# Raw fp32 weights in place of split halves for the second block's projections: a two-block transformer kernel on one Trainium2 core

## Chip, cores and metric

The kernel runs on one core of one Trainium2 chip. The metric is the device time of one execution in microseconds (us). The engines are called as in the profile: PE is TensorE's matmul stream and PEld its weight loads, DVE is VectorE, ACT ScalarE, POOL GpSimd, and SP the queue of SyncE, which issues the loads of the weights.

## What is computed

A batch of one sequence of 256 tokens with 1024 features goes through two different blocks, all in float32. The first block has two layers of attention and a convolved, gated MLP. The second block normalises its input and projects it with one wide matrix, `w_in_2`, and everything that follows in it reads slices of that product:

```python
xn = rmsnorm(h, norm1_g[layer])
proj = xn @ w_in[layer]
u, q, k, v, qi, ki, wi, g_ssm, g_attn = jnp.split(proj, offsets, axis=-1)
y_ssm = s5_branch(u, ...)              # a linear recurrence over the tokens, 512 features
y_attn = dsa_branch(q, k, v, qi, ki, wi)   # attention over keys chosen by an index score
merged = sigmoid(g_ssm) * (y_ssm @ w_ssm_up) + sigmoid(g_attn) * (y_attn @ w_attn_up)
h = h + merged @ w_out
h = h + peer_ffn(rmsnorm(h, norm2_g), ...)   # product-key routing to 16384 experts
```

The widths of the slices are 512 (u), 512 + 128 + 128 (q, k, v), 256 + 32 + 8 (qi, ki, wi) and twice 1024 (the gates).

## The kernel before

**Units.** Every weight matrix is cut into units of 128 x 1024 float32 (512 KB), listed in `plan` in the order of use. A unit has a slot, `i % 6`, with three buffers of SBUF: `raw` (what SP loads), `wh` and `wl`. ACT copies `raw` into `wh` as float32r (L953), and DVE (L1284) or POOL (L1941) writes the rest, `raw - wh`, into `wl`; the table `lower` says which of the two. The activations have the same two halves: after a transposition on PE, ACT copies the bank into `hh`, and DVE subtracts (L1290) into `hl`. `mm3` (L507) then multiplies each pair with three float32r matmuls: high by high, high by low, low by high.

**Who waits for whom.** SP loads unit i into `raw` when the unit six places ahead has had its low half made (L470 on). ACT writes `wh` again when PE has used the unit six places ahead. The three engines that split do it inside their own programs, in order: each `stream(i)` in such a program is the place where it splits the units that have come free, and what stands behind it on the engine waits too.

**The stage around the change.** It runs in the profile from about 720 to 900 us. First come the two RMS norms between the blocks (DVE at L1639 and L1650, roots on POOL), the transposition `turned(("n", 2), ...)` (L523) and `by_features("u", ...)`: 4 units, each of 8 products with 256 moving columns. DVE prepares `Br`, PE turns it (L745), and DVE and ACT copy it into `BT`. Then a loop over n = 0 to 15 does the recurrence, one step for 32 features. In its step n PE does `state_in(n + 1)` (L498, four records with 32 rows), `state_out(n - 1)` (L780, eight records), some transpositions of queries and index scores (n = 7 to 11), and then `FILL[n]` units of the projections `wqkv` (8 units), `wqk` (one unit, 16 products of 40 columns) and `wga` (16 units). A unit of `wqkv` or `wga` holds four products with 512 moving columns. Three units are left for after the loop, and `state_out(15)` stands behind them.

```python
FILL = [2, 2, 2, 2, 2, 2, 1, 2, 1, 1, 1, 1, 1, 1, 1, 0]
for n in range(16):
    if n + 1 < 16:
        state_in(n + 1)
    if n:
        state_out(n - 1)
    ...
    for _ in range(FILL[n]):
        next(fill)
run(fill)
state_out(15)
```

In step n DVE multiplies the bank of `state_in(n)` with a table, adds, and runs two scans (L1734); POOL multiplies the result (`ssb` or `ssv`, L1946), and that is what `state_out(n)` waits for. At n = 5 DVE also rotates queries and keys (`rope`, four products and two sums) and POOL the index queries, and from n = 10 DVE chooses keys (`chosen`, L1301, L1712, L1714). Behind its step DVE makes the low halves of as many units as `FILL[n]` says. ACT copies the finished projections out of their banks. After the stage, at 900.89 us, the attention over the chosen keys begins with a matmul on `qT`.

Of the kernel before, what the change touches and what calls it, by code (L numbers as in the profile page):

```python
# [8 lines left out]
F32R = mybir.dt.float32r  # L9
# [79 lines left out]
def tcols(t):  # L89
    return slice(t * 128, (t + 1) * 128)  # L90
# [5 lines left out]
def program(nc, x_d, pos_d, consts_d, smalls_d, win_d, wout_d, wup_d, wdown_d, rows_d, wu_d, wqkv_d, wqk_d, wga_d, wsm_d,  # L96
            wglu_d, wsu_d, wau_d, wout2_d, wpq_d, keys_d, ut_d, vt_d, out_d, spill_d):
    with ExitStack() as ctx:

        def scoped(where, name, n, dt=F32):  # L100
            return where.enter_context(nc.sbuf_tensor(name, [128, n], dt))
# [13 lines left out]
        whs += [scoped(early, f"wh{i}", 1024, F32R) for i in (4, 5)]  # L115
        wls += [scoped(early, f"wl{i}", 1024, F32R) for i in (4, 5)]
# [47 lines left out]
        def stage(name, units):  # L164
            first[name] = len(plan)
            plan.extend(units)

        def quarters(w):
            return [(w[:, h * 1024:h * 1024 + 1024], 1024, True) for h in range(w.shape[1] // 1024)]


        WOUT = [(0, 0), (0, 1), (1, 0), (1, 1), (0, 2), (1, 2), (0, 3), (1, 3)]
# [7 lines left out]
            stage(("wdown", L), [(wdown_d[L, f], 1024, True) for f in range(NTILE)])  # L180
        stage(("row", "g"), [(rows_d[4], 1024, False)])
        stage(("row", "n", 2), [(rows_d[5], 1024, False)])
        stage("wu", [(wu_d[n], 1024, True) for n in range(4)])
        stage("wqkv", quarters(wqkv_d[0]) + quarters(wqkv_d[1]))
        stage("wqk", [(wqk_d, 320, True)])
        stage("wga", sum([quarters(wga_d[n]) for n in range(4)], []))
        stage("wglu", [(wglu_d[n], 1024, True) for n in range(2)])
        stage("wsu", quarters(wsu_d[0]) + quarters(wsu_d[1]))
        stage("wau", quarters(wau_d[0]) + quarters(wau_d[1]))
# [28 lines left out]
        J_GATE, N_GR = 57, 64  # L218


        normed = [first["wup", L] for L in range(DEPTH)] + [first["win", 1], first["wu"], first["wpq"]]


        lower = []
        for i in range(n_units):
            d2 = first["wga"] - 8 <= i < first["wglu"]
            if i < 6:
                lower.append("pd"[i % 2])
            elif first["ut"] <= i < first["ut"] + J_GATE:
                lower.append("p")  # L230
            elif first["ut"] <= i < first["vt"]:
                lower.append("d")
            elif any(u <= i < u + 4 for u in normed):
                lower.append("p")
            elif i >= first["ut"]:
                lower.append("dp"[i % 2])
            elif i >= first["wpq"]:
                lower.append("dp"[i % 2])
            elif i >= first["wglu"]:
                lower.append("p")  # L240
            elif d2:
                lower.append("d")
# [20 lines left out]
        def lo_out(i):  # L263
            return dve_lo if lower[i] == "d" else pool_lo

        def unit_pair(i, k, kt, cols):
# [8 lines left out]
        hTl = hl[:, :].rearrange("p (k t) -> p k t", k=8)  # L275
        hn2 = att[:, 0:2048].rearrange("p (t d) -> p t d", t=2)
        cosT = tab_s[:, 0:4096].rearrange("p (n t) -> p n t", n=16)
        sinT = tab_s[:, 4096:8192].rearrange("p (n t) -> p n t", n=16)
# [14 lines left out]
        def hT(k, cols):  # L293
            return hTh[:, k, cols], hTl[:, k, cols]
# [189 lines left out]
        def pe(p):  # L484
# [31 lines left out]
            def turned(st, src, ncol, ts, after, of=range(8)):  # L516
                for t in ts:
                    for q in range(ncol // 4):
# [6 lines left out]
                        bank_of["T", st, t, q] = b  # L525
                        emptied[b] = (dve_out, ("hT", st, t, q))

            def by_tokens(tag, u0, n_slabs, cw, nu, kper, off, ready, empties, of=range(8), skew=(), between=None):
                for n in range(n_slabs):
                    bs = [rot(of), rot(of)]  # L530
                    order = [(h, t) for h in range(nu) for t in range(2)]
                    if n in skew:
                        order.sort(key=lambda ht: ht[1])
                    for h, t in order:
                        i, b = u0 + n * nu + h, bs[t]
                        if t == 0:
                            unit(i)
                        elif n in skew and h == 0 and between:
                            between()
                        if h == 0:  # L540
                            claim(b)
                        m = mm3(banks[b][:, 0:cw], [hT(off + h * kper + k, tcols(t)) for k in range(kper)],
                                [unit_pair(i, k, kper, slice(0, cw)) for k in range(kper)], h == 0, h == nu - 1,
                                lambda k: ready(t, h * kper + k))
                        if h == nu - 1:
                            bank_of[tag, n, t] = b
                            emptied[b] = empties(n, t)
                            m.then_inc(pe_out.up(("mm", tag, n, t), ("used", i) if t else None), 1)
                        elif t:
                            m.then_inc(pe_out.up(("used", i)), 1)  # L550
                        if t:
                            yield

            def by_features(tag, u0, n_slabs, kt, c2, off, ready, empties):
                for n in range(n_slabs):
                    i = u0 + n
                    unit(i)
                    for c in range(c2):
                        b = rot()
                        claim(b)  # L560
                        m = mm3(banks[b][:, 0:256], [unit_pair(i, k, kt, tcols(c)) for k in range(kt)],
                                [hT(off + k, ALLC) for k in range(kt)], True, True, ready)
# [7 lines left out]

            def ready_tokens(st):
                return lambda t, k: p.wait_ge(dve_out, ("hT", st, t, k // 4))

            def ready_both(st):
                return lambda k: p.wait_ge(dve_out, ("hT", st, 0, k // 4), ("hT", st, 1, k // 4))
# [173 lines left out]
            low, side = [0, 1, 2, 3], (2, 3)  # L749

            def projections():
                yield from by_tokens("wqkv", first["wqkv"], 2, 512, 4, 2, 0, ready_tokens(("n", 2)), lambda n, t: (act_out, ("ev", "wqkv", n, t)), of=low)
                yield from by_tokens("wqk", first["wqk"], 1, 40, 1, 8, 0, ready_tokens(("n", 2)), lambda n, t: (act_out, ("ev", "wqk", n, t)), of=low)
                low[:] = [0, 1]
                yield from by_tokens("wga", first["wga"], 4, 512, 4, 2, 0, ready_tokens(("n", 2)), lambda n, t: (act_out, ("ev", "wga", n, t)), of=low)

            fill = projections()

# [177 lines left out]
        def act(a):  # L936
# [335 lines left out]
        def dve(v):  # L1272
# [958 lines left out]
```

## Time and profile before

| | us |
|---|---|
| median of 3 runs | 1850.11 |
| lowest, highest | 1848.39, 1851.78 |
| time of the profiled execution | 1850.76 |
| its span (first to last instruction) | 1849.0 |
| PE busy | 1736.3 (94%) |
| DVE busy | 1192.5 (64%) |
| ACT busy | 870.2 (47%) |
| POOL busy | 744.6 (40%) |

The busy time of PE counts overlapping matmuls once, and each matmul's time includes its way through the array, so the time from one start to the next is the cost in a stream, and not the duration of one. A float32 matmul shows in the trace as two records.

### The profile page before, as it was taken

The numbers are of one execution on the slowest core, as the hardware profiler recorded it, in microseconds if no ns is written. First come the engines' busy times: TensorE is split into PE (matmuls) and PEld (weight loads), VectorE is DVE, ScalarE is ACT, GpSimd is POOL, SyncE is SP. The second block draws the span as 40 slices with busy tenths as digits, with TensorE's granted clock in tenths as the row PEclk, the third lists the DMA queues.
The fourth block names the chain that finished last, engine by engine and source line by source line (L and its number), as shares of the span: only waits on it lengthen the run. The fifth ranks groups of instructions, "written<-read, shape, count | busy, mean of one in ns | idle before, by whom it ended". The sixth has DMA issues, their size and how long they took to land.

```text
span 1849.0 us, 27364 instructions
## 1 busy us (share of the span) xinstructions
PE 1736.3 (94%) x10744; PEld 1513.6 (82%) x10744; DVE 1192.5 (64%) x2462; ACT 870.2 (47%) x1508; POOL 744.6 (40%) x398
## 2 busy tenths in 40 slices
PE   6998999989989998988788999989999999999997
PEld 4776999867679986765567999989999988888886
DVE  7453674745447666677653399989999844444444
ACT  5544566344456654222444355544444445555553
POOL 2323578043236752232445399830000044444442
PEclk9998999999999998989899999999999999999998
DMA  7231555553235565422134365644444456666664
GB/s 277 88 106 67 186 185 166 185 183 103 92 114 191 175 193 179 134 81 67 57 114 159 113 208 172 194 138 146 140 144 142 160 171 193 194 193 194 193 194 136
DMA packets 77456, 283.21 MB, mean 153 GB/s; under 512 B 8720, under 2 KB 8976, under 8 KB 77072
## 3 DMA queue, kind: packets, MB, share of 16 engines
q1 hardware_dynamic: 76032, 276.50, 46.2%
q10 hardware_dynamic: 1296, 4.97, 0.7%
q8 instruction: 85, 1.39, 0.3%
q14 instruction: 43, 0.35, 0.1%
HBM read 279.33 MB, written 2.10 MB: 152 GB/s over the span
## 4 chain that ended last, share of the span: by engine, by line
PE 76%; DVE 15%; issue 3%; ACT 3%; POOL 2%; DMA 1%; POOLq 0%; DVEq 0%; ACTq 0%
PE bank L507 66%; PE bank L498 7%; DVE H L1290 2%; POOL wl L1941 2%; PE bank L590 1%; DVE H L1815 1%; DVE H L1821 1%; DVE H L1817 1%; ACT wh L953 1%; DVE H L1819 1%; DVE H L1813 1%; PE bank L780 1%; DVE gates L1290 1%; DVE ssb L1290 1%; DVE wl L1284 1%
## 5 line engine op out<-in xcount | busy, mean ns | idle before, releaser
L1941 POOL TENSOR_TENSOR wl<-raw,wh 128x1024 fp32r<-128x1024 f32 x227 | 579.6, 2564 | 729.7 <-ACT wh L953 714.7
L953 ACT ACTIVATE wh<-raw 128x1024 fp32r<-128x1024 f32 x515 | 532.6, 1048 | 109.8 <-PE bank L507 99.8
L507 PE MATMUL bank<-hh,wh 128*128 128x256 f32 x1904 | 546.5, 287 | 5.8 <-DVE hl L1290 3.1
L507 PE MATMUL bank<-hl,wh 128*128 128x256 f32 x1904 | 538.5, 283 | 0.0
L507 PE MATMUL bank<-hh,wl 128*128 128x256 f32 x1904 | 537.0, 282 | 0.0
L1284 DVE TENSOR_TENSOR wl<-raw,wh 128x1024 fp32r<-128x1024 f32 (+1 forms) x288 | 382.9, 1335 | 144.8 <-ACT wh L953 144.7
L507 PEld LDWEIGHTS bank<-hh,wh 128*128 128x128 f32 x1904 | 364.5, 191 | 8.1 <-POOL wl L1941 5.6
L507 PEld LDWEIGHTS bank<-hl,wh 128*128 128x128 f32 x1904 | 364.6, 192 | 0.0
L507 PEld LDWEIGHTS bank<-hh,wl 128*128 128x128 f32 x1904 | 364.1, 191 | 0.0
L1290 DVE TENSOR_TENSOR acl<-H,ach 128x256 fp32r<-128x256 f32 x128 | 87.6, 685 | 183.2 <-ACT ach L956 183.2
L507 PE MATMUL bank<-wh,ach 128*128 128x512 f32 x512 | 200.0, 391 | 1.9 <-DVE acl L1290 1.9
L507 PE MATMUL bank<-wl,ach 128*128 128x512 f32 x512 | 199.9, 390 | 0.0
L507 PE MATMUL bank<-wh,acl 128*128 128x512 f32 x512 | 199.7, 390 | 0.0
L507 PE MATMUL bank<-wh,hh 128*128 128x512 f32 (+1 forms) x432 | 180.4, 418 | 9.8 <-DVE hl L1290 5.3
L956 ACT ACTIVATE H<-bank 128x256 f32<-128x256 f32 (+33 forms) x197 | 64.5, 327 | 247.6 <-PE bank L507 215.1
L507 PE MATMUL bank<-wl,hh 128*128 128x512 f32 (+1 forms) x432 | 172.3, 399 | 0.0
L507 PE MATMUL bank<-wh,hl 128*128 128x512 f32 (+1 forms) x432 | 172.2, 399 | 0.0
L956 ACT ACTIVATE ach<-H 128x256 fp32r<-128x256 f32 x128 | 53.4, 418 | 174.3 <-PE bank L507 173.8
L1301 DVE SCALAR_TENSOR_TENSOR att<-bank,sml,att 128x255 f32<-128x255 f32 (+1 forms) x176 | 84.5, 480 | 62.5 <-ACT att L956 59.4
L507 PEld LDWEIGHTS bank<-wh,ach 128*128 128x128 f32 x512 | 96.4, 188 | 22.4 <-issue 2.1
L507 PEld LDWEIGHTS bank<-wh,hh 128*128 128x128 f32 x432 | 84.6, 196 | 35.6 <-issue 11.6
L507 PEld LDWEIGHTS bank<-wh,acl 128*128 128x128 f32 x512 | 96.5, 189 | 20.2
(203 smaller groups left out, 2289.1 us busy)
## 6 DMA issues: line engine op xcount, KB each, us to landing
raw<-in_ut_dram SPq DMA_DIRECT2D x128, 512.0 KB, 3.5
raw<-in_vt_dram SPq DMA_DIRECT2D x128, 512.0 KB, 3.7
raw<-in_wup_dram SPq DMA_DIRECT2D x88, 512.0 KB, 4.0
raw<-in_win_dram SPq DMA_DIRECT2D x48, 512.0 KB, 4.5
raw<-in_wdown_dram SPq DMA_DIRECT2D x44, 512.0 KB, 4.1
raw<-in_wout_dram SPq DMA_DIRECT2D x24, 512.0 KB, 3.6
raw<-in_wga_dram SPq DMA_DIRECT2D x16, 512.0 KB, 3.5
raw<-in_wpq_dram SPq DMA_DIRECT2D x16, 512.0 KB, 3.6
```

Of the source, the lines that this page charges most:

```text
L498: m = p.e.matmul(out, l, r, start=i == 0, stop=i == len(pairs) - 1)
L507: m = p.e.matmul(out, lhs[i][a], rhs[i][b], start=start and i == 0 and j == 0, stop=stop and i == n - 1 and j == 2)
L590: m = p.e.transpose(banks[b][:, 128 * k:128 * k + 128], buf[:, 1024 + 256 * (i % NB) + 128 * k:1152 + 256 * (i % NB) + 128 * k], ids[:, :])
L780: m = p.e.matmul(banks[yb][o:o + 32, 0:256], l[:, 32 * n:32 * n + 32], s, start=j == 0, stop=j == 3, tile_position=(0, o))
L953: a.e.activation(high_of(u), raw_of(u), ACTF.Copy).then_inc(act_hi.up(("hi", u)), 1)
L956: a.e.activation(out, src, f, **kw).then_inc(act_out.up(ev), 1)
L1284: v.e.tensor_tensor(low_of(u), raw_of(u), high_of(u).bitcast(F32), ALU.subtract).then_inc(dve_lo.up(("lo", u)), 1)
L1290: v.e.tensor_tensor(out, a, b, op).then_inc(dve_out.up(ev), 1)
L1301: v.e.scalar_tensor_tensor(out, a, s, b, op0, op1).then_inc(dve_out.up(ev), 1)
L1813: v.e.max(values[:, 0:8], s_).then_inc(dve_out.up(), 1)
L1815: v.e.max_index(index[:, 0:8], values[:, 0:8], s_).then_inc(dve_out.up(), 1)
L1941: g.e.tensor_tensor(low_of(u), raw_of(u), high_of(u).bitcast(F32), ALU.subtract).then_inc(pool_lo.up(("lo", u)), 1)
```

## The change

The 29 units of `wu`, `wqkv`, `wqk` and `wga` are no longer split. PE multiplies `raw` itself, in float32, with the whole activation, which stands in a new buffer `hw` (view `hTw`). Each product is one float32 matmul in place of three float32r ones: 144 in place of 432. ACT's copies into `wh` and DVE's and POOL's subtractions of these units go away. Of the four copies of the activation from its banks, ACT does the two of the first half of the features and DVE the two of the second, without waiting for each other. A raw buffer of these units is free for the next load when PE has used the unit, not when it has been split. To make room, `hw` lies over `wh4` and `wl4`, and the slots are shifted by two so that slot 4 fits this. All other weights are split as before.

```diff
-            whs += ... (4, 5); wls += ... (4, 5)
...
+        whs += [scoped(sc_h, "wh4", 1024, F32R), wh5]
+        wls += [scoped(sc_h, "wl4", 1024, F32R), wl5]
+        sc_h.close()
+        hw = scoped(early, "hw", 2048)
...
-        stage("wu", [(wu_d[n], 1024, True) for n in range(4)])
-        stage("wqkv", quarters(wqkv_d[0]) + quarters(wqkv_d[1]))
-        stage("wqk", [(wqk_d, 320, True)])
-        stage("wga", sum([quarters(wga_d[n]) for n in range(4)], []))
+        stage("wu", [(wu_d[n], 1024, False) for n in range(4)])
+        stage("wqkv", quarters(wqkv_d[0], False) + quarters(wqkv_d[1], False))
+        stage("wqk", [(wqk_d, 320, False)])
+        stage("wga", sum([quarters(wga_d[n], False) for n in range(4)], []))
...
-        slot = [i % 6 if i < n_early else (i - n_early) % 4 for i in range(n_units)]
+        slot = [(i + 2) % 6 if i < n_early else (i - n_early) % 4 for i in range(n_units)]
...
         def used_by(i):
-            return dve_out if plan[i][0] is not None and not plan[i][2] and not first["keys"] <= i < n_early else pe_out
+            whole = first["wu"] <= i < first["wglu"] or first["keys"] <= i < n_early
+            return pe_out if plan[i][2] or whole else dve_out
...
+            def turned_whole(st, src):
...
+                        emptied[b] = (dve_out if q else act_out, ("hT", st, t, q))
...
+                            for k in range(kper):
+                                ready(t, h * kper + k)
+                                m = p.e.matmul(banks[b][:, 0:cw], hTw[:, off + h * kper + k, tcols(t)], unit_whole(i, k, kper, slice(0, cw)),
+                                               start=h == 0 and k == 0, stop=h == nu - 1 and k == kper - 1)
...
+                            for k in range(kt):
+                                ready(k)
+                                m = p.e.matmul(banks[b][:, 0:256], unit_whole(i, k, kt, tcols(c)), hTw[:, off + k, ALLC], start=k == 0, stop=k == kt - 1)
...
-            turned(("n", 2), hn2, 8, (0, 1), lambda t: (dve_out, ("nrm", ("n", 2), t)))
-            by_features("u", first["wu"], 4, 8, 1, 0, ready_both(("n", 2)), lambda c: (act_out if c % 2 else dve_out, ("ev", "u", c)))
+            turned_whole(("n", 2), hn2)
+            by_features("u", first["wu"], 4, 8, 1, 0, ready_whole_both(("n", 2)), lambda c: (act_out if c % 2 else dve_out, ("ev", "u", c)))
...
-            turned(("n", 2), (0, 1), 2)
+            for t in range(2):
+                a.wait_ge(pe_out, ("T", ("n", 2), t, 0))
+                do(hTw[:, 0:4, tcols(t)], quad(ps("T", ("n", 2), t, 0)), ACTF.Copy, ("hT", ("n", 2), t, 0))
...
-            turned(("n", 2), (0, 1), 2)
+            for t in range(2):
+                v.wait_ge(pe_out, ("T", ("n", 2), t, 1))
+                copy(hTw[:, 4:8, tcols(t)], quad(ps("T", ("n", 2), t, 1)), ("hT", ("n", 2), t, 1), alone=True)
```

## Rows read from the trace of the kernel before

**Rows 1.** The page: busy us of each engine, share, instructions.

```profile
PE 1736.3 (94%) x10744; PEld 1513.6 (82%) x10744; DVE 1192.5 (64%) x2462; ACT 870.2 (47%) x1508; POOL 744.6 (40%) x398
```

**Rows 2.** Windows: length, busy PE, PEld, DVE, ACT, POOL, granted clock, DMA share, GB/s.

```profile
750.00:760.00 10.00, 10.00 (x33) 7.37 (x34) 6.02 (x8) 1.06 (x1) 3.28 (x1) 0.66 0.38 116
750.00:900.00 150.00, 135.88 (x575) 90.74 (x576) 110.12 (x171) 38.99 (x58) 51.31 (x23) 0.93 0.24 75
```

**Rows 3.** The chain of waits from 720 to 752 us: start, us, what.

```profile
722.15 5.66 POOL wl L1941 x2
...
731.03 1.13 PE bank L523 x4
...
732.82 0.70 DVE hl L1290
...
733.65 12.93 PE bank L507 x96
...
747.97 1.23 DVE wl L1284
...
749.90 1.76 PE bank L498 x8
```

**Rows 4.** Timeline of DVE around the norms: start, us, instruction, [idle before].

```profile
717.14 1.22 DVE L1639 TENSOR_TENSOR mix<-xs,raw 128x1024 f32<-128x1024 f32 x1
...
723.30 2.30 DVE L1639 TENSOR_TENSOR mix<-xs,raw 128x1024 f32<-128x1024 f32 x1
725.70 0.15 DVE L1295 TENSOR_SCALAR sta<-sta 128x1 f32<-128x1 f32 x1
```

**Rows 5.** Timeline of PE in the stage, the same columns.

```profile
763.58 0.39 PE L507 MATMUL bank<-wh,hh 128*128 128x512 f32 x1
...
765.91 0.40 PE L507 MATMUL bank<-wl,hh 128*128 128x512 f32 x1
...
788.98 0.27 PE L507 MATMUL bank<-wl,hh 128*128 128x40 f32 x1
...
794.12 0.27 PE L507 MATMUL bank<-wh,hl 128*128 128x40 f32 x1
...
873.09 1.03 PE L780 MATMUL bank<-ssb,cw 128*32 128x256 f32 x2 [3.27 <-POOL ssb L1946]
...
900.89 0.49 PE L498 MATMUL bank<-qT 64*128 64x128 f32 x4
```

**Rows 6.** The chain of waits: pieces of PE in step n = 4, and one later.

```profile
780.22 5.80 PE bank L507 x24
786.02 1.06 PE bank L498 x4
787.07 1.84 PE bank L780 x8
...
1412.63 0.89 PE bank L498 x8
```

**Rows 7.** Groups of PE, 750 to 900 us: busy us, mean ns, idle before.

```profile
L498 PE MATMUL bank<-qT 32*128 32x128 f32 x16 | 2.5, 296 | 0.1
L498 PE MATMUL bank<-qT 32*128 32x256 f32 x16 | 2.3, 400 | 0.0
L794 PE MATMUL bank<-ids,proj 128*128 128x128 f32 x12 | 2.2, 327 | 0.0
L794 PE MATMUL bank<-ids,tab 128*128 128x128 f32 x6 | 1.3, 340 | 0.0
```

**Rows 8.** Waits between 700 and 900 us: us in total, times, longest.

```profile
DVE wl L1284 <- ACT wh L953: 35.3, 10, 6.9
```

**Rows 9.** Timeline of DVE: product of n = 10, scans of n = 15.

```profile
849.54 1.22 DVE L1290 TENSOR_TENSOR ssb<-bank,tab 128x1024 f32<-128x1024 f32 x1
...
894.86 1.27 DVE L1734 TENSOR_TENSOR_SCAN ssv<-sta,ssb 128x256 f32<-128x256 f32 x2
```

**Rows 10.** Groups of DVE, 750 to 900 us, the same columns as Rows 7.

```profile
L1284 DVE TENSOR_TENSOR wl<-raw,wh 128x1024 fp32r<-128x1024 f32 x19 | 24.3, 1288 | 28.9 <-ACT wh L953 28.9
```

**Rows 11.** The page, DMA issues: KB each, median us from issue to landing.

```profile
raw<-in_wqkv_dram SPq DMA_DIRECT2D x8, 512.0 KB, 6.3
```

More of the change, by code:

```diff
@@ L114, in program @@
         raws += [scoped(early, f"raw{i}", 1024) for i in (4, 5)]
[L115 to L116 removed]
+        wh5, wl5 = scoped(early, "wh5", 1024, F32R), scoped(early, "wl5", 1024, F32R)
+        sc_h = ExitStack()
+        whs += [scoped(sc_h, "wh4", 1024, F32R), wh5]
+        wls += [scoped(sc_h, "wl4", 1024, F32R), wl5]
+        sc_h.close()
+        hw = scoped(early, "hw", 2048)
         sc_l = ExitStack()
@@ L166, in stage, with quarters @@
             plan.extend(units)
-        def quarters(w):
-            return [(w[:, h * 1024:h * 1024 + 1024], 1024, True) for h in range(w.shape[1] // 1024)]
+        def quarters(w, split=True):
+            return [(w[:, h * 1024:h * 1024 + 1024], 1024, split) for h in range(w.shape[1] // 1024)]
         WOUT = [(0, 0), (0, 1), (1, 0), (1, 1), (0, 2), (1, 2), (0, 3), (1, 3)]
@@ L218, in program @@
         J_GATE, N_GR = 57, 64
-        normed = [first["wup", L] for L in range(DEPTH)] + [first["win", 1], first["wu"], first["wpq"]]
+        normed = [first["wup", L] for L in range(DEPTH)] + [first["win", 1], first["wpq"]]
         lower = []
         for i in range(n_units):
-            d2 = first["wga"] - 8 <= i < first["wglu"]
             if i < 6:
@@ L526, in turned @@
                         emptied[b] = (dve_out, ("hT", st, t, q))
+            def turned_whole(st, src):
+                for t in range(2):
+                    for q in range(2):
+                        b = rot()
+                        claim(b)
+                        p.wait_ge(dve_out, ("nrm", st, t))
+                        for k in range(4):
+                            m = p.e.transpose(banks[b][:, k * 128:k * 128 + 128], src[:, t, (4 * q + k) * 128:(4 * q + k + 1) * 128], ids[:, :])
+                        m.then_inc(pe_out.up(("T", st, t, q)), 1)
+                        bank_of["T", st, t, q] = b
+                        emptied[b] = (dve_out if q else act_out, ("hT", st, t, q))
             def by_tokens(tag, u0, n_slabs, cw, nu, kper, off, ready, empties, of=range(8), skew=(), between=None):
@@ L541, in by_tokens @@
                             claim(b)
-                        m = mm3(banks[b][:, 0:cw], [hT(off + h * kper + k, tcols(t)) for k in range(kper)],
-                                [unit_pair(i, k, kper, slice(0, cw)) for k in range(kper)], h == 0, h == nu - 1,
-                                lambda k: ready(t, h * kper + k))
+                        if plan[i][2]:
+                            m = mm3(banks[b][:, 0:cw], [hT(off + h * kper + k, tcols(t)) for k in range(kper)],
+                                    [unit_pair(i, k, kper, slice(0, cw)) for k in range(kper)], h == 0, h == nu - 1,
+                                    lambda k: ready(t, h * kper + k))
+                        else:
+                            for k in range(kper):
+                                ready(t, h * kper + k)
+                                m = p.e.matmul(banks[b][:, 0:cw], hTw[:, off + h * kper + k, tcols(t)], unit_whole(i, k, kper, slice(0, cw)),
+                                               start=h == 0 and k == 0, stop=h == nu - 1 and k == kper - 1)
                         if h == nu - 1:
@@ L560, in by_features @@
                         claim(b)
-                        m = mm3(banks[b][:, 0:256], [unit_pair(i, k, kt, tcols(c)) for k in range(kt)],
-                                [hT(off + k, ALLC) for k in range(kt)], True, True, ready)
+                        if plan[i][2]:
+                            m = mm3(banks[b][:, 0:256], [unit_pair(i, k, kt, tcols(c)) for k in range(kt)],
+                                    [hT(off + k, ALLC) for k in range(kt)], True, True, ready)
+                        else:
+                            for k in range(kt):
+                                ready(k)
+                                m = p.e.matmul(banks[b][:, 0:256], unit_whole(i, k, kt, tcols(c)), hTw[:, off + k, ALLC], start=k == 0, stop=k == kt - 1)
                         bank_of[tag, c2 * n + c] = b
@@ L572, in ready_tokens, with whole_at, ready_whole, ready_whole_both @@
                 return lambda t, k: p.wait_ge(dve_out, ("hT", st, t, k // 4))
+            def whole_at(st, t, q):
+                p.wait_ge(dve_out if q else act_out, ("hT", st, t, q))
+            def ready_whole(st):
+                return lambda t, k: whole_at(st, t, k // 4)
+            def ready_whole_both(st):
+                return lambda k: (whole_at(st, 0, k // 4), whole_at(st, 1, k // 4))
             def ready_both(st):
@@ L751, in projections @@
             def projections():
-                yield from by_tokens("wqkv", first["wqkv"], 2, 512, 4, 2, 0, ready_tokens(("n", 2)), lambda n, t: (act_out, ("ev", "wqkv", n, t)), of=low)
-                yield from by_tokens("wqk", first["wqk"], 1, 40, 1, 8, 0, ready_tokens(("n", 2)), lambda n, t: (act_out, ("ev", "wqk", n, t)), of=low)
+                yield from by_tokens("wqkv", first["wqkv"], 2, 512, 4, 2, 0, ready_whole(("n", 2)), lambda n, t: (act_out, ("ev", "wqkv", n, t)), of=low)
+                yield from by_tokens("wqk", first["wqk"], 1, 40, 1, 8, 0, ready_whole(("n", 2)), lambda n, t: (act_out, ("ev", "wqk", n, t)), of=low)
                 low[:] = [0, 1]
-                yield from by_tokens("wga", first["wga"], 4, 512, 4, 2, 0, ready_tokens(("n", 2)), lambda n, t: (act_out, ("ev", "wga", n, t)), of=low)
+                yield from by_tokens("wga", first["wga"], 4, 512, 4, 2, 0, ready_whole(("n", 2)), lambda n, t: (act_out, ("ev", "wga", n, t)), of=low)
             fill = projections()
@@ L1657, in dve @@
                 stream(first["row", "n", 1] if L == 0 else first["row", "g"])
-            turned(("n", 2), (0, 1), 2)
+            for t in range(2):
+                v.wait_ge(pe_out, ("T", ("n", 2), t, 1))
+                copy(hTw[:, 4:8, tcols(t)], quad(ps("T", ("n", 2), t, 1)), ("hT", ("n", 2), t, 1), alone=True)
             for t in range(2):
```

6 lines of the change are left out of this document (4 added, 2 removed).

## Prediction

> **What bounds the kernel now.** I read the page first. PE is busy for 94% of the span [rows 1], so a change to its work moves the end wherever PE is the last to be waited for. Then the windows: in the stage of the second block's projections PE is busy for 135.9 of 150 us, the granted clock averages 0.93, and in the first 10 us it is 0.66 [rows 2]. The stage thus has some 14 us of idle PE and a few at the lower of its two clocks. Then the chain of waits, for what ends those idle times. Ahead of the stage the chain passes through two subtractions on POOL (5.66 us), later through DVE's low half of the activation and, at 747.97, through a low half of a weight that stands ahead of `BT` on DVE [rows 3]. Inside the loop PE waits for POOL's product of the recurrence, as before 873.09 for 3.27 us [rows 5]; POOL waits for DVE, and DVE stood in its order behind low halves that waited for ACT, 35.3 us in ten waits [rows 8]. The reader is to see a stage where PE's own work, and waits made by the splitting, take turns at setting the end.
>
> **What the change costs on PE.** A float32r matmul of 512 columns follows the last one in (765.91 - 763.58) / 10 = 0.233 us [rows 5], so a product of three costs 0.699. With 256 columns it is 3 x 0.118 = 0.354: 96 records in 12.93 us, of which the first were at the low clock; 0.118 is the step that leaves 83 of them for the time after the clock rose. With 40 columns 46 steps take 5.14 us, 0.112 each or 0.335 a product [rows 5].
>
> What a float32 product of 512 columns costs, no row shows. Two rows have float32 with fewer columns: four products of 128 columns in 0.89 us, 0.2225 each, and four times that for 512 columns, 0.89; and four products of 256 columns in 1.84 us, 0.46 each, 0.92 for 512 columns [rows 6]. The second has gaps between its operands' switches in it, so I take 0.89 and keep 0.92. The lower bound is four streams of 512 columns at 2.4 GHz without any gap, 0.853; the upper one four times the float32r step, 0.933. For 256 columns half of that: 0.445 (0.427 to 0.47). For 40 columns the trace has only the step of 0.11 us per record, which both the row of 128 columns (0.111) and that of 40 (0.112) show; two records make 0.222.
>
> So PE gets 96 x (0.89 - 0.699) = 18.3 us more in the large products, 32 x (0.445 - 0.354) = 2.9 more in `wu`, and 16 x (0.335 - 0.222) = 1.8 less in `wqk`: 19.4 us more.
>
> The Trainium skill says under "FP8 and Floating Point Precision", section "TensorE Precision Notes", that true FP32 takes four passes through the array. The rows agree (0.2225 us for 128 columns is 4.2 times 128 columns at 2.4 GHz). By this rule, on PE alone, four passes in place of three float32r matmuls speak against the change, and it would end slower; that case is the last of the rivals below.
>
> **What it gives back, part by part.** *Ahead of the transposition.* POOL no longer makes two low halves from 722.15 [rows 3]. The root behind them could start once DVE's 725.70 instruction is done; POOL came to it at about 727.8. That is 1.9 us. DVE's product took 2.30 us beside them, and 1.22 without [rows 4], another 1.1, of which ACT's sum of squares behind it leaves most. I take 2.8 of at most 3.0: the transpositions begin at 728.2 in place of 731.03.
>
> *The activation.* Before, ACT's copy and then DVE's subtraction (0.70 us) stood between the transposition and the first product; now there is one copy, and the second half is another engine's. The eight transpositions last 2.0 us at the low clock, so the first product starts at 730.25 in place of 733.65: 3.4 us in all [rows 3].
>
> *`wu`.* PE stays at the low clock for about as long as before after it starts again, so I put 3.6 us of the 32 products there, which does 4.1 of them; 27.9 x 0.445 = 12.4 follow. It ends at 746.3, against 733.65 + 12.93 = 746.6 before: the front's gain pays for the fourth pass, no more.
>
> *`BT`.* The low half at 747.97 and ACT's copy of a weight ahead of it are gone. DVE's and ACT's copies of `BT` can follow the two groups of transpositions, and `state_in(0)` starts 1.75 us after `wu` instead of 3.3: at 748.1. It is 749.9 when the first unit can start, if the clock stays up.
>
> *The loop.* Now PE's own work sets it, added up: 14 `state_in` at 1.06, 14.8; 16 `state_out` at 1.84, 29.4 [rows 6]; transpositions of queries and index scores, 2.5 + 2.3 + 2.2 + 1.3 = 8.3 [rows 7]; 24 units of four products, 96 x 0.89 = 85.4; `wqk` 16 x 0.222 = 3.6. Between the blocks of a step I add 0.15 us, 16 times, 2.4: 24 records take 5.80 us where 24 steps make 5.59 [rows 5, 6]. The sum is 143.9, and the stage ends at 893.8. Before, it ended at 900.89 [rows 5]. The gain is 7.1 us.
>
> *Is anything else late?* Of DVE's 110.1 us in these 150 [rows 2], 24.3 are low halves [rows 10], and its waits for ACT's high halves go with them. The densest part is from the product of n = 10 to the scans of n = 15, 46.6 us [rows 9], with four low halves of 1.22 in it: about 41.7. Counted back from 893.8 (nine units 32.0, eight `state_out` 14.7, six `state_in` 6.4, index scores and transpositions 5.4, gaps 1.0), PE starts step 9 at 834.3 and has `state_in(10)` done at 835, so with some 5 us of waits for the index scores DVE has its last scan done at 882, POOL 2.4 later, and PE asks for it at 892. That is 7 us of cover. If it were gone, each us beyond it would be on the path. ACT's copies out of the banks are unchanged; behind the last of them it splits one unit, loads a table and does the Gelu, as before, so the attention behind the stage moves as a whole.
>
> *The loads.* A raw buffer is now held until PE has used it. SP's queue is in order, and behind each waiting load stand all the later ones. Five units of at least 3.56 us, 17.8, lie between the release and the use, against 6.3 us to land [rows 11]. So the queue costs nothing. The last units of `wga` release the raw buffers of the first split units behind the stage; the last needed early is loaded 3.6 us before PE ends, ACT splits it where it did. The shift of the slots moves the last two early units off the slots of the expert weights, whose first four loads can come sooner; there the chain goes through DVE's routing, which has the same work, so I put that at nothing. POOL has no low half of these units in the loop before either, so its products keep their time.
>
> **The time.** The sum stands against the profiled execution, 1850.76 with a span of 1849.0; this is within 0.7 us of the median, 1850.11. So 1850.1 - 7.1 = 1843.0.
>
> **Rivals.**
> *The low clock stays at the front (10%).* In the first 10 us of the loop the clock was 0.66, behind the pause of 3.3 us between `wu` and `state_in(0)` that only transpositions break [rows 2, 3]. I expect it to stay up behind one of 1.75. For this rival: the transpositions and the matmuls with 32 rows around the pause are the same. At the low clock until 757, 7 us of work would take twice the time: 3.5 us lost, and 1846.5.
>
> *The price is high (15%).* At 0.933 the large products cost 96 x 0.043 = 4.1 us more and `wu` 0.7: 1847.8, and no difference to be told. For it: the float32r stream itself runs 9% over its columns. Against: the float32 row of 128 columns is only 4% over.
>
> *The price is low and the gaps between the blocks go (12%).* The 0.15 us between blocks may come from the change between float32r and float32, which is gone. With 0.87 a product that makes 1.9 + 2.4 us less, 1838.7.
>
> *Slower (16%): DVE's and POOL's own work still sets the recurrence.* The step at n = 5 has DVE's rotation, and n = 11 to 15 the choice of keys; if PE's waits for POOL were due to these and not to the low halves in front, the loop's idle time of about 14 us would stay, PE's 19.4 us would come on top, and only the front's 3.4 and 1.8 us and the clock's 2.5 come back: 1850.1 + 19.4 - 7.7 = 1861.8. For it: DVE is far the busiest beside PE. It decides as soon as PE asks for the product of n = 14 or 15 before POOL has it, that is when DVE needs over 7 us more than I counted; half of that idle time kept would already end slower.
>
> **How the numbers follow.** About 0.2% (3.7 us) is what a measurement of this kernel can tell from no change. My own case has 47%, with 1840 to 1846 as its own range. It, the low price and half of the case with the low clock are faster: 0.64. The high price and the other half are the same: 0.20. The last rival is slower: 0.16. The likeliest time is 1843. The range goes from 1837, under the low price, to 1852, past the high price with the low clock on top (1851.3); the far part of the last rival is left out.
>
> **What would show it.** The new matmuls stand as two records with 512 columns, some 0.445 us from start to start; over 0.465 the price was wrong. In the loop PE should have almost no wait for POOL, and steps 1 to 3 should be 10.0 us long in place of 8.7, with the end of the stage at 893 to 894. The transpositions ahead should begin near 728. The granted clock from 750 to 760 should be 1.00. If PE waits for L1946 from n = 11 on, the last rival has it. If the stage ends where I say and the whole does not, something behind it took the gain: the loads of the split units, or the routing.

## The result, and the profile after

| | before | after |
|---|---|---|
| median of 4 runs, us | 1850.74 | 1834.44 |
| lowest, highest | 1848.39, 1851.78 | 1832.88, 1837.33 |
| profiled execution, its span | 1850.76, 1849.0 | 1832.88, 1830.9 |

The ratio is 0.9914 with an interval of 0.9902 to 0.9926: the kernel is 15.9 us faster (13.7 to 18.1); the medians differ by 16.3. The forecast was 1843.0 with a range of 1837 to 1852. The sign was right, and so was the way in which the gain comes about; but the gain was more than twice the 7.1 us of the forecast, and the time lies 2.6 us outside the range.

The page of the changed kernel, engines and shares of the chain that ended last:

```profile
PE 1740.5 (95%) x10600; PEld 1488.1 (81%) x10600; DVE 1155.3 (63%) x2435; ACT 842.4 (46%) x1477; POOL 728.6 (40%) x394
PE 80%; DVE 12%; issue 2%; ACT 2%; POOL 2%; DMA 1%; POOLq 0%; ACTq 0%; DVEq 0%
```

PE is busy for 4.2 us longer than in [rows 1] while the span is 18.1 us shorter: PE does more work and waits less.

The waits of PE between 720 and 890 us (us in total, times, longest). The loop had waits for POOL's product; now there is none:

```profile
PE bank L545 <- DVE att L1694: 5.2, 2, 4.9
PE bank L507 <- DVE sta L1501: 2.1, 1, 2.1
PE bank L507 <- ACT BT L998: 0.8, 1, 0.8
```

The chain of waits (start, us, what) from the norms to the end of the stage, against [rows 3, 6]. L545 is the transposition, L595 `wu`, L787 the turn of `Br`, L507 `state_in`, L571 the units of the loop, L822 `state_out`:

```profile
726.50 1.97 PE bank L545 x8
728.47 15.38 PE bank L595 x64
743.85 0.89 PE bank L787 x8
...
744.76 0.61 ACT BT L998
...
745.50 1.14 PE bank L507 x8
746.64 7.06 PE bank L571 x16
753.71 1.06 PE bank L507 x4
754.76 1.84 PE bank L822 x8
756.61 7.06 PE bank L571 x16
...
786.50 7.20 PE bank L571 x40
...
868.99 3.63 PE bank L571 x8
872.62 1.84 PE bank L822 x8
874.46 10.51 PE bank L571 x24
```

From 746.64 on, the chain stays on PE but for two short copies of ACT at 831.66 and 833.05: block follows block, which is what "bound by PE" looks like in this view. The price of a product comes out of it. One unit (8 records, four products) takes 3.63 us, three units in a row 10.51: two further units cost 6.88, so a product costs 0.860 us and not 0.89. What is left of the single unit, 3.63 - 3.44 = 0.19, is paid once for a block that follows matmuls with 32 rows or 32 columns (`state_in`, `state_out`): the two blocks that follow a transposition with all 128, at 813.90 and 824.70, take 6.87 and 3.44 and don't pay it.

The windows have the clock (the columns of [rows 2]). It was 0.66 from 750 to 760 and 0.93 over the stage:

```profile
750.00:760.00 10.00, 10.00 (x29) 4.42 (x28) 7.62 (x10) 0.00 (x0) 6.25 (x3) 1.00 0.34 105
750.00:893.00 143.00, 138.75 (x461) 65.66 (x459) 88.63 (x162) 27.40 (x48) 56.57 (x27) 1.00 0.32 100
```

The groups of PE from 720 to 895 us (busy, mean ns | idle before):

```profile
L571 PE MATMUL bank<-raw,hw 128*128 128x512 f32 x192 | 86.4, 600 | 0.0
...
L595 PE MATMUL bank<-hw,raw 128*128 128x256 f32 x64 | 15.5, 406 | 0.0
...
L571 PE MATMUL bank<-raw,hw 128*128 128x40 f32 x32 | 3.8, 283 | 0.0
```

**Where the 18.1 us between the two spans are.** Four landmarks are in both traces: DVE's first sum of the residual ahead of the norms (715.65 before, 713.93 after), the first matmul on `qT` (900.89, 886.73), DVE's last copy of the expert scores out of a bank (1054.96, 1039.63), and the turn of the first selection of experts (1220.42, 1203.46). The third column is the changed kernel once more, the profile of e6 below, with a span of 1832.9.

| stretch, us | before | after | after, e6 |
|---|---|---|---|
| start to first sum | 715.65 | 713.93 | 716.71 |
| the stage, to `qT` | 185.24 | 172.80 | 172.47 |
| attention, to the last score copy | 154.07 | 152.90 | 152.62 |
| routing, to the first selection | 165.46 | 163.83 | 163.57 |
| the rest | 628.6 | 627.4 | 627.5 |

The first line is chance: nothing in it was changed but the numbers of the slots, and the same kernel gives 713.93 and 716.71. The stage gives 12.4 to 12.8 us, where 7.1 were forecast. Behind it come 1.2 to 1.5, then 1.6 to 1.9 in a part that the prediction put at nothing, and about 1.1 in the rest.

### The profile page after: what moved, and what is told of

Same layout as the page of the kernel before. It is cut to its first block, busy times and chain, and to the rows that moved or that the text cites. A ratio compares the mean times of both kernels' runs of the same rounds, so it can differ in the third digit from the quotient of the medians.

```text
span 1830.9 us, 27000 instructions
## 1 busy us (share of the span) xinstructions
PE 1740.5 (95%) x10600; PEld 1488.1 (81%) x10600; DVE 1155.3 (63%) x2435; ACT 842.4 (46%) x1477; POOL 728.6 (40%) x394
## 4 chain that ended last, share of the span: by engine, by line
PE 80%; DVE 12%; issue 2%; ACT 2%; POOL 2%; DMA 1%; POOLq 0%; ACTq 0%; DVEq 0%
PE bank L516 62%; PE bank L507 8%; PE bank L571 5%; DVE H L1334 2%; PE bank L822 2%; POOL wl L1987 1%; PE bank L632 1%; DVE H L1867 1%; DVE H L1861 1%; DVE H L1863 1%; DVE H L1859 1%; DVE H L1865 1%; PE bank L595 1%; ACT wh L995 1%; DVE gates L1334 1%
## 5 line engine op out<-in xcount | busy, mean ns | idle before, releaser
L1987 POOL TENSOR_TENSOR wl<-raw,wh 128x1024 fp32r<-128x1024 f32 x223 | 568.3, 2557 | 727.6 <-ACT wh L995 715.9
L995 ACT ACTIVATE wh<-raw 128x1024 fp32r<-128x1024 f32 x486 | 503.7, 1051 | 79.8 <-PE bank L516 63.7
L516 PE MATMUL bank<-hh,wh 128*128 128x256 f32 x1872 | 535.9, 286 | 3.6 <-POOL wl L1987 2.3
L516 PE MATMUL bank<-hl,wh 128*128 128x256 f32 x1872 | 528.5, 282 | 0.0
L516 PE MATMUL bank<-hh,wl 128*128 128x256 f32 x1872 | 527.2, 282 | 0.0
L1328 DVE TENSOR_TENSOR wl<-raw,wh 128x1024 fp32r<-128x1024 f32 x263 | 352.9, 1347 | 110.6 <-ACT wh L995 110.3
L516 PE MATMUL bank<-wh,hh 128*128 128x512 f32 x320 | 134.3, 420 | 9.2 <-DVE hl L1334 5.3
L516 PE MATMUL bank<-wl,hh 128*128 128x512 f32 x320 | 128.3, 401 | 0.0
L516 PE MATMUL bank<-wh,hl 128*128 128x512 f32 x320 | 127.9, 400 | 0.0
L516 PEld LDWEIGHTS bank<-wl,ach 128*128 128x128 f32 x512 | 96.1, 188 | 20.0
```

The lines of the kernel that those rows point to most:

```text
L995: a.e.activation(high_of(u), raw_of(u), ACTF.Copy).then_inc(act_hi.up(("hi", u)), 1)
L1328: v.e.tensor_tensor(low_of(u), raw_of(u), high_of(u).bitcast(F32), ALU.subtract).then_inc(dve_lo.up(("lo", u)), 1)
L1987: g.e.tensor_tensor(low_of(u), raw_of(u), high_of(u).bitcast(F32), ALU.subtract).then_inc(pool_lo.up(("lo", u)), 1)
```

## The experiments

Eight kernels ran, each timed against the kernel before on the same chip. That kernel's median is 1850.4 beside e1, e3, e4 and e5, and 1849.77 beside e2, e6, e7 and e8.

**e1: the shift of the slots alone.**

```diff
-        slot = [i % 6 if i < n_early else (i - n_early) % 4 for i in range(n_units)]
+        slot = [(i + 2) % 6 if i < n_early else (i - n_early) % 4 for i in range(n_units)]
```

> The kernel before with the slots shifted by two and nothing else. Theory A (the shift frees the first expert loads from the last two early units, so POOL's backlog of low halves at the start of the expert stage goes, and DVE's routing, which sets the end there, meets POOL less often): 1.5 to 2.5 us faster than before, and the first matmul on the selected experts 1.5 us nearer to the end of the score matmuls than 165.5 us. Theory B (the 1.6 us between the two traces there are chance, or come with the change's other timing): within 0.7 us of before.

Measured: 1848.21 (12 runs), ratio 0.9984 (0.9976 to 0.9993), 3.0 us faster by the ratio (1.3 to 4.4) and 2.2 by the medians; routing takes 163.78 (1055.80 to 1219.58) in place of 165.46. The shift is a gain by itself, and 1.7 us of it are in the routing. All the traces agree on that: routing takes 163.5 to 163.8 us in the six with the shift (e1, e2, e3, e6, e8 and the changed kernel) and 164.9 to 165.5 in the four without. About 1.0 more may be in the rest of the kernel, which takes 627.4 to 627.7 in four of the six and 628.3 to 628.6 in the four, but 629.0 in e2 and e3.

The stage of this trace is 3.0 us longer than before (188.26, from 713.07 to 901.33), though nothing in it was changed but the numbers of the slots. 2.7 of them are in one block, the one of `wqk` with its 40 columns, where the granted clock was lower with PE busy all the time (the columns of [rows 2], then the chain):

```profile
786.28:794.44 8.16, 8.16 (x50) 8.16 (x50) 3.02 (x5) 0.20 (x1) 2.36 (x1) 0.65 0.24 67
786.28 8.16 PE bank L507 x48
```

In the kernel before the same 48 records take 5.48 us at 1.00. A single trace of this kernel can thus hide a gain of 3 us, or feign one.

How it works is read from two timelines (start, us, instruction, [idle before]). POOL in the changed kernel makes the expert stage's low halves from 1029 on and then one by one, each waiting 0.4 us for ACT:

```profile
1029.14 4.75 POOL L1987 TENSOR_TENSOR wl<-raw,wh 128x1024 fp32r<-128x1024 f32 x2 [7.91 <-ACT wh L995]
...
1061.55 2.40 POOL L1987 TENSOR_TENSOR wl<-raw,wh 128x1024 fp32r<-128x1024 f32 x1 [0.40 <-ACT wh L995]
1064.35 2.40 POOL L1987 TENSOR_TENSOR wl<-raw,wh 128x1024 fp32r<-128x1024 f32 x1 [0.40 <-ACT wh L995]
```

In the changed kernel without the shift (e4) it waits longer first and then has eleven of them back to back:

```profile
1034.94 2.36 POOL L1985 TENSOR_TENSOR wl<-raw,wh 128x1024 fp32r<-128x1024 f32 x1 [13.57 <-ACT wh L993]
1042.30 2.37 POOL L1985 TENSOR_TENSOR wl<-raw,wh 128x1024 fp32r<-128x1024 f32 x1 [5.00 <-ACT wh L993]
1045.28 26.18 POOL L1985 TENSOR_TENSOR wl<-raw,wh 128x1024 fp32r<-128x1024 f32 x11 [0.61 <-ACT wh L993]
```

DVE's routing runs beside them. Its first instruction of 2048 columns comes in the changed kernel 0.01 us ahead of POOL's next, and then POOL's takes 4.55 us in place of 2.40:

```profile
1069.94 2.29 DVE L1334 TENSOR_TENSOR H<-H 128x2048 f32<-128x2048 f32 x1
1069.95 4.55 POOL L1987 TENSOR_TENSOR wl<-raw,wh 128x1024 fp32r<-128x1024 f32 x1 [0.40 <-ACT wh L995]
```

In e4 it starts while one of POOL's is running, and DVE pays:

```profile
1069.06 2.40 POOL L1985 TENSOR_TENSOR wl<-raw,wh 128x1024 fp32r<-128x1024 f32 x1
1070.09 3.52 DVE L1332 TENSOR_TENSOR H<-H 128x2048 f32<-128x2048 f32 x1
```

The two take turns: POOL's ends at 1071.46, and from there to DVE's end at 1073.61 are 2.15 us, about the 2.29 that DVE's takes when it is first. POOL's next one, from 1071.86, takes 4.01. In the kernel before DVE's takes 4.18 us, in e1 2.29. Which of DVE's instructions meet POOL's differs from trace to trace: the ten of 2048 columns add up to 41.5 us before and 37.5 in e1, to 38.8 in e4, and to 37.6 in the changed kernel, but to 39.7 in e6, whose routing is no longer for it. So these ten show how the slowing comes about, and not the whole of the 1.7 us. DVE's work is the same, as the prediction said; its time is not.

**e4: the change without the shift.** `hw` lies over `hh`, so the slots can stay.

```diff
-        slot = [(i + 2) % 6 if i < n_early else (i - n_early) % 4 for i in range(n_units)]
+        slot = [i % 6 if i < n_early else (i - n_early) % 4 for i in range(n_units)]
...
-        hw = scoped(early, "hw", 2048)
...
-        hh, hl = scoped(ctx, "hh", 2048, F32R), scoped(ctx, "hl", 2048, F32R)
+        sc_h = ExitStack()
+        hh = scoped(sc_h, "hh", 2048, F32R)
+        sc_h.close()
+        hw = scoped(ctx, "hw", 2048)
+        hl = scoped(ctx, "hl", 2048, F32R)
```

> The changed kernel with the slots not shifted; the whole activation stands over the high half of the activation instead of over a weight buffer, which is free then. Theory A: 1.5 to 2.5 us slower than the changed kernel, 1836 to 1837. Theory B: equal to it within 0.7 us, 1834.4.

Measured: 1837.99, ratio 0.9931 (0.9918 to 0.9945), 12.8 us faster than before and 3.1 slower than with the shift by the ratios (3.6 by the medians); its median is 1 us above the 1836 to 1837 that theory A had. Routing is 164.88 (1039.79 to 1204.67). The two intervals overlap, but e1 found a gain of 2 to 3 us from the other side. So the float32 part alone is worth some 13 us, and the shift some 2 to 3.

**e3: float32 products, but the halves are still made and waited for.** `wu`, `wqkv`, `wqk` and `wga` keep their splitting on ACT, DVE and POOL, PE waits for it, and multiplies `raw`.

```diff
-                        if plan[i][2]:
+                        if not whole(i):
...
-        stage("wu", [(wu_d[n], 1024, False) for n in range(4)])
+        stage("wu", [(wu_d[n], 1024, True) for n in range(4)])
```

(and so for the other three; `hw` lies over `hh` as in e4, but the slots are shifted as in the changed kernel)

> The changed kernel's float32 products, with all the splitting of the 29 units kept on ACT, DVE and POOL, and PE waiting for the low half before it multiplies the raw unit (the halves are not used; the activation stands where its high half stood). So the price on PE is paid and the queues are as before. Theory of the prediction (the change wins by what it takes off the queues, and PE's price of 18 us is real): slower than before, 1855 to 1866. Rival (the gain comes from the matmuls themselves, by fewer instructions and a steadier clock, and the splitting was covered): faster than before, 1834 to 1845.

Measured: 1859.39, ratio 1.0046 (1.0034 to 1.0058), 8.5 us slower. The waits of PE are back:

```profile
PE bank L826 <- POOL ssb L1996: 10.1, 4, 4.2
```

The products and the slots are those of the changed kernel, and it is 25.0 us slower by the medians: the gain is in what the other engines no longer have to do, and not in the products. What float32 costs by itself this run doesn't tell cleanly, for two reasons. It has the shift's gain in it, so that beside the kernel before the rest costs some 11.5 us and not 8.5. And PE reads `raw` here, so `raw` is held until PE has used it, as in the changed kernel, but it has still to be split after it lands. ACT's copies waited 45.8 us for the loads of `wga` and `wqkv` between 750 and 910 us, where the kernel before has 0.4 between 700 and 900, and the loop's chain passes through two landings:

```profile
796.42 3.59 DMA raw<-in_wga_dram
...
833.28 4.02 DMA raw<-in_wga_dram
```

So part of the loss is due to these late loads, which neither of the two kernels has to wait for.

**e5: the kernel before, without the low halves of the 29 units.** The products use the high half twice.

```diff
+        for i in range(first["wu"], first["wglu"]):
+            lower[i] = "n"
...
-            return wls[slot[i]][:, 0:plan[i][1]]
+            return whs[slot[i]][:, 0:plan[i][1]] if lower[i] == "n" else wls[slot[i]][:, 0:plan[i][1]]
```

> The kernel before without the low halves of the 29 units: three float32r products as before, but the high half stands in for the low one, and PE waits for ACT's copy alone (the result lacks these low halves). So the queues of DVE and POOL are freed and PE pays nothing. Theory of the prediction: the gain of the queues without the price, and then DVE is the bound from n = 10 on: 1822 to 1830, clearly under the changed kernel. Rival (the low halves on DVE were not what PE waited for): 1840 or more.

Measured: 1827.89, ratio 0.987 (0.9853 to 0.9887), 24.1 us faster. No wait of PE for POOL is left in its loop. This is what the subtractions, and the loads held back by them, cost in the kernel before, with ACT's copies kept. Without the shift, as here, the changed kernel gains 12.8 us (e4): the 11.3 between the two runs are left for PE's dearer products, which come to 16 us by their prices (96 x 0.161 + 32 x 0.075 - 16 x 0.11, with half of 0.860 taken for 256 columns). The trace of this run was at the lower clock in the block of `wqk` and the one behind it (60 records, 11.53 us at 0.70), which its time has in it too.

**e7: the kernel before, with the loop's low halves on POOL.** The other way to free DVE, at no price on PE.

```diff
             elif d2:
-                lower.append("d")
+                lower.append("p")
...
+                projections(FILL[n])
-            for _ in range(25):
-                projections(1)
+            projections(first["wglu"] - fill[0])
```

> The kernel before with the low halves of wqkv, wqk and wga made by POOL, behind its product of each step, and not by DVE: three float32r products, DVE's queue free. Theory A (DVE's queue was what PE waited for, and POOL has room for 24 times 2.4 us): faster than before by 8 to 20 us, so near the changed kernel or under it, 1830 to 1842. Theory B (POOL is then late with its product of the recurrence, the one thing that PE waits for, and slows DVE beside it): no faster than before, 1850 to 1870.

Measured: 1852.1 (11 runs), ratio 1.0012 (1.0003 to 1.0021): no gain. PE waits as before, in fewer places, and `state_in(0)` waits longer for `BT`:

```profile
PE bank L780 <- POOL ssb L1946: 11.3, 3, 4.4
...
PE bank L498 <- DVE BT L1306: 4.6, 1, 4.6
```

Around PE's first wait two low halves stand in front of POOL's product, and POOL goes from one to the next without a wait:

```profile
812.27 5.29 POOL L1941 TENSOR_TENSOR wl<-raw,wh 128x1024 fp32r<-128x1024 f32 x2
817.53 2.51 POOL L1946 TENSOR_TENSOR ssb<-ssv,tab 128x1024 f32<-128x1024 f32 x1
820.10 1.06 PE L780 MATMUL bank<-ssb,cw 128*32 128x256 f32 x2 [4.24 <-POOL ssb L1946]
```

DVE's scan ahead of that product was done at 812.86. Not every product is late by them: those at 765.45, 772.57 and 781.24 start after POOL has waited 0.6 to 1.2 us for DVE. The low halves on POOL slow DVE as well: ahead of the loop two `TENSOR_SCALAR` of 512 columns, on the way to `BT`, take 2.42 and 2.46 us in place of 0.43 each.

The low halves cost about the same on either engine, as both are in the recurrence. They had to go, not to move.

**e2: one more product in each of the 24 units of the loop.**

```diff
+                                if cw == 512 and t and k == 0:
+                                    m = p.e.matmul(banks[b][:, 0:cw], hTw[:, off + h * kper + k, tcols(t)], unit_whole(i, k, kper, slice(0, cw)),
+                                                   start=False, stop=False)
```

> The changed kernel with one float32 product of 512 columns more in each of the 24 units of wqkv and wga (it is added to the sum once more, so these projections are not the reference's). Theory A (PE's own stream sets the stage from end to end, and a product costs 0.883 us): 24 x 0.883 = 21.2 us more than the changed kernel, 1855 to 1856. Theory B (DVE's choice of keys is the bound from n = 11 on, and covers part): 12 to 18 us more.

Measured: 1857.21, ratio 1.0035 (1.0021 to 1.0048), 22.8 us more than the changed kernel's 1834.44 by the medians. 24 x 0.86 is 20.6. The chain has the added product's own line, L574:

```profile
750.00 0.86 PE bank L574 x2
750.86 3.43 PE bank L571 x8
754.29 0.86 PE bank L574 x2
```

It confirms the price of 0.86, and that nothing but PE sets the loop now: what is added to it comes out at the end in full. Eight records between two others take 3.43, without the 0.19 of a block. (The 0.883 expected had that 0.19 spread over the products: 7.06 / 8.) The 2.2 us beyond 20.6 can be the clock: in this trace the stage is 25.9 us longer (198.69), and 5.1 of them are two places at the lower clock, at `wqk` and the block behind it (793.95 to 803.45 at 0.66, then 1.07 for one added product) and at 851.02 (4.47 us for the 2.77 of the other blocks). How often this happens beyond the one trace is not known.

**e8: `wu` split as before, the loop in float32.** The activation then exists in both forms.

```diff
-        stage("wu", [(wu_d[n], 1024, False) for n in range(4)])
+        stage("wu", [(wu_d[n], 1024, True) for n in range(4)])
...
-            by_features("u", first["wu"], 4, 8, 1, 0, ready_whole_both(("n", 2)), lambda c: ...
+            by_features("u", first["wu"], 4, 8, 1, 0, ready_both(("n", 2)), lambda c: ...
```

> The changed kernel with wu split as before (ACT and POOL make its halves, PE multiplies it in float32r, and the activation stands in both forms), the other 25 units whole. Theory A (ahead of the loop the change gives back about as much as wu's fourth pass costs, 3 us against 2.5): within 1.5 us of the changed kernel. Theory B (wu is where the gain beyond the forecast came from): 4 us or more slower than the changed kernel.

Measured: 1837.65 (five runs, 1831.93 to 1838.08), ratio 0.992 (0.9905 to 0.9934). By the ratio that is 0.9 us slower than e6's 0.9915, by the medians 3.3, and its stage takes 176.46 (716.25 to 892.71), 3.7 to 4.0 more. Two of its runs are as quick as the changed kernel's, so the times don't decide between the theories. The trace says that the first unit starts 34.68 us after the first sum and not 32.71, with POOL's two subtractions back in the chain: 2.0 us of the 3.7. The other 1.7 are the block with `wqk`, 8.90 us at a granted clock of 0.81 in place of 7.20 at 1.00, which splitting `wu` need not have caused, as e1, e2 and e5 have it too.

**e6: the changed kernel once more,** beside e2, e7 and e8, with no edit.

> The changed kernel once more, as the mark for the others of this call, and for what differs from one execution to the next in stretches that the change doesn't touch: 0.991 of before. In the trace the stage's lengths should come back within 0.3 us, whichever clock the first block had; where the first block is 1 to 2 us longer or shorter, the granted clock around 125 to 145 us should say so.

Measured: 1834.39, ratio 0.9915 (0.9901 to 0.9928): the result repeats, and its profile gave the third column above. The stage came back within 0.33 us (172.47 against 172.80). Its first part is 2.8 us longer, and the granted clock from 125 to 145 us is 0.91 in place of 1.00, as was expected of a longer one; but e8 has 1.00 there and 716.25, so the clock of that stretch is not all of it.

## Why the prediction was right, and where it failed

**Right: what the splitting cost.** The prediction said that waits made by the splitting took turns with PE at setting the end, and that without them PE's own work would. The loop has no wait for POOL, the steps n = 1 to 3 take 9.96 us each (10.0 forecast; 753.71 to 763.67 is the first), and the transposition ahead begins 12.57 us after the first sum (12.55 forecast, 728.2 - 715.65). e3 and e5 show the two sides: +8.5 us for float32 where the halves are kept (with the shift and the late loads in it), -24.1 for the halves. The rival on the slower side, that DVE's and POOL's own work sets the recurrence, did not come: with the halves gone that work stays in full, and PE waits for none of it in the loop. One row was read too wide: the 35.3 us of [rows 8] are from 700 to 900 us, and 28.9 of them are in the 150 us of the loop [rows 10]; no term of the sum used it.

**The step that failed: the sum of the stage, and first of all its price of a product.** In the frame of the kernel before (715.65 for the first sum) the forecast has 178.15 us from there to `qT`; it took 172.80. Term by term:

| term | forecast | measured | too much |
|---|---|---|---|
| first sum to the first product of `wu` | 14.60 | 14.54 (728.47 - 713.93) | 0.06 |
| `wu` | 16.05 | 15.38 | 0.7 |
| `wu` to the first unit: `BT`, `state_in(0)`, `state_in(1)` | 3.6 | 2.79 (743.85 to 746.64) | 0.8 |
| 96 products | 85.4 | 96 x 0.86 = 82.6 | 2.8 |
| `wqk` | 3.6 | 7.20 - 3.63 = 3.57 | 0.0 |
| between blocks (16 at 0.15; 14 pay 0.19) | 2.4 | 2.6 | -0.2 |
| queries and index scores | 8.3 | 7.1 | 1.2 |
| `state_in`, `state_out` | 44.2 | 44.3 | -0.1 |

The 2.6 is what the chain's pieces of L571 (88.7 us in all) leave after 82.6 and 3.57. The sum of the last column is 5.3, which is the stage's whole surplus. The term of `wu` has the same price in it (27.9 x 0.015 = 0.4 of its 0.7), and it moves with the clock at its start: 15.06 us in e6 and 14.86 in e4.

*The price.* 0.89 was the row of four products of 128 columns, eight records in 0.89 us, taken as one product of 512 columns, two records. The columns are the same, 0.853 us at 2.4 GHz, but what each record takes beyond its columns, (0.89 - 0.853) / 8 = 0.005 us, came in eight times in place of twice. With twice it would have been 0.862; 0.860 was measured. So the row held the right price and the scaling was wrong, if what a record takes beyond its columns is the same for 128 columns as for 512; the numbers fit that, and no run varied it. The Trainium skill's rule of four passes for true FP32 ("FP8 and Floating Point Precision", "TensorE Precision Notes") is borne out: 0.860 is 1.01 times four passes of 512 columns at 2.4 GHz. The float32r stream is 9% over its columns, and the rival with the high price had taken that over to float32.

*The clock.* From the end of `wu` to the first unit it was 5.1 us (746.58 to 751.66), at the low clock at its end, and is 2.8 now, at 1.00, and the eight matmuls of `state_in` from 1.76 us to 1.14. The prediction had counted 3.6 for the two together. In the loop of the kernel before, the lower clock follows two of PE's three waits for POOL of over 3 us, those that end at 820.30 and 873.09, and not the one that ends at 888.61 (the columns of [rows 2]):

```profile
818.00:826.00 8.00, 5.70 (x18) 3.26 (x19) 4.01 (x6) 0.95 (x3) 4.59 (x2) 0.57 0.22 68
873.50:876.00 2.50, 2.50 (x7) 1.05 (x6) 2.47 (x3) 0.00 (x0) 0.00 (x0) 0.50 0.08 29
888.50:891.00 2.50, 2.39 (x10) 1.28 (x11) 2.32 (x6) 0.00 (x0) 0.05 (x1) 1.00 0.00 0
```

A third place has no wait: in or just behind the 40 columns of `wqk`, with PE busy throughout, the clock was lower in seven of the ten traces, and at 1.00 in the changed kernel, e4 and e6. What decides it no run shows.

*Queries and index scores.* The 8.3 was read as busy time, partly at the low clock and with neighbours overlapping in PE; as pieces of the chain, from one block's start to the next one's, they take 0.81 + 1.02 + 0.60 + 2.57 + 1.07 + 1.07 = 7.1.

**The second failure: the shift "at nothing".** The routing "has the same work", which is right, but low halves that POOL makes back to back beside it slow DVE. e1 puts the shift at 3.0 us (1.3 to 4.4), and the traces find 1.6 to 1.9 of it in the routing and perhaps 1.0 behind it. The stage's surplus alone gives 1837.7 and the shift alone 1840.0, both inside the range; together they give 1834.7, outside it.

**Behind the stage** attention is 1.2 to 1.5 us shorter. The prediction had it move "as a whole". It is not the shift: e1 has 154.47 there, e4 152.47. Nor is it the splitting: e3, which keeps it, has 152.52, and e5, without low halves, 153.94. It goes with the float32 products: 151.9 to 152.9 us in all six traces that have them, 153.9 to 154.5 in the four that don't. PE's waits add up to 17.8 us in place of 18.9, and the clock of the first 39.1 us is 0.83 in place of 0.78, but e2 has 151.87 with 0.78 there. Why stays open.

**The rivals.** The low price was half right: the price was under 0.87, the gaps between blocks stayed. The low clock at the front and the high price did not come.

## What to carry to other kernels

Count a split for the engines that make it: here three float32r passes saved 0.16 us of PE per product over float32, and their low halves cost 24 us of the kernel's time (e5), as DVE and POOL had a recurrence in the same queue. Take the price of a long instruction from differences between blocks of the same kind, not from a short one times its length, and keep what a block pays once apart. When a wait of PE goes, look what the clock did behind it, and when loads move, look which engines run beside each other afterwards.

## What the runs showed of the hardware

- A float32 matmul of 512 columns costs 0.860 us in a stream, 0.86 when one is added (e2), against 0.699 for the three float32r ones: 1.23 times, not 1.33 times, since float32r loses 9% over its columns and float32 1%.
- DVE's and POOL's tensor_tensor with both inputs in SBUF took turns, and the one that started first lost nothing: 128 x 2048 on DVE took 2.29 us when it was 0.01 ahead, and POOL's 4.55 for 2.40; behind POOL's it took 3.52 (e4) and 4.18 (before). 1.22 and 2.30 in [rows 4] are another such pair.
- Between matmuls with 32 rows or columns and those with 128, a float32 block paid 0.19 us; behind other matmuls with 128 it paid nothing.
- The granted clock fell to its lower level also where PE never waited, at the 40 columns of `wqk` (0.65 over 8.16 us in e1, 1.00 for the same work in the kernel before). It cost up to 3 us, in some traces and not in others.
- Two executions of the same kernel differ by 2.8 us before the stage (713.93 and 716.71), as much as the shift is worth. A part of this size can be told by stretches between landmarks, or by a dozen runs, not by a single time.
